# First layer of a hybrid decoder step: a third of the tokens runs ahead through the first feed-forward, and VectorE does the whole depthwise convolution

## The reference

```python
def swiglu(h, wg, wu, wd):
    return (jax.nn.silu(h @ wg) * (h @ wu)) @ wd

def conformer_conv(h, hist, w_pw1, b_pw1, w_dw, b_dw, ln_g, ln_b, w_pw2, b_pw2):
    u = h @ w_pw1 + b_pw1
    g = u[..., :D_CONV] * jax.nn.sigmoid(u[..., D_CONV:])
    gh = jnp.concatenate([hist.astype(g.dtype), g], axis=1)
    new_hist = gh[:, -CONV_HIST:]
    c = causal_dwconv(gh, w_dw, b_dw)          # 31 taps, each channel by itself
    c = jax.nn.silu(layernorm(c, ln_g, ln_b))
    return c @ w_pw2 + b_pw2, new_hist

# trunk, per layer i
    hn = rmsnorm(h, norm_mix[i])
    ... mix = conformer_conv(hn, ...) if i is even, ssd_mixer(hn, ...) if odd
    h = h + mix
    h = h + swiglu(rmsnorm(h, norm_ffn[i]), ffn_w_gate[i], ffn_w_up[i], ffn_w_down[i])
```

## Time and profile before

| what | value |
|---|---|
| median of 3 runs | 3497.72 us (3488.77 to 3501.15) |
| the profiled execution | 3490.01 us, its span 3488.1 us |
| PE busy | 3325.2 us, 95% of the span |
| DVE, ACT, POOL busy | 1591.4 (46%), 872.0 (25%), 934.1 us (27%) |
| granted TensorE clock, mean | 0.978 of full speed |
| read from memory | 131.39 MB |

### The profile page before, as it was taken

How to read it: one execution, slowest core, us unless ns; L and a number is a source line. 1 busy time by engine, 2 the same in 40 slices (tenths; PEclk the granted TensorE clock), 3 DMA queues, 4 the chain that set the end, 5 groups by cost and what they waited for, 6 DMA issues and landing times.

```text
span 3488.1 us, 52341 instructions
## 1 busy us (share of the span) xinstructions
PE 3325.2 (95%) x19646; PEld 3156.8 (91%) x19646; DVE 1591.4 (46%) x2619; ACT 872.0 (25%) x1570; POOL 934.1 (27%) x733
## 2 busy tenths in 40 slices
PE   4899969999999999998999999999979999999998
PEld 3888749999999999887999999999978999999998
DVE  3299962232222322646566575575654223222234
ACT  2111042211111111433333333333333111111113
POOL 2221122321111211413333334343333221112110
PEclk8999989999999999988999999999999999999999
DMA  3001001111111111110211211211111111111111
GB/s 99 25 25 30 18 5 41 43 42 46 44 42 42 42 48 42 43 46 11 59 45 36 63 50 37 63 32 49 48 35 31 42 42 48 42 42 42 44 46 58
DMA packets 226995, 147.24 MB, mean 42 GB/s; under 512 B 7796, under 2 KB 208852, under 8 KB 226866
## 3 DMA queue, kind: packets, MB, share of 16 engines
q1 hardware_dynamic: 226757, 145.96, 14.2%
q10 hardware_dynamic: 173, 0.39, 0.1%
HBM read 131.39 MB, written 15.65 MB: 42 GB/s over the span
## 4 chain that ended last, share of the span: by engine, by line
PE 83%; issue 6%; DVE 6%; ACT 2%; POOL 1%; DMA 1%; SPq 0%; DVEq 0%; POOLq 0%; ACTq 0%
PE bank L535 69%; PE bank L525 2%; PE bank L636 2%; PE bank L875 2%; PE bank L561 1%; PE bank L880 1%; PE bank L881 1%; PE bank L912 1%; PE bank L918 1%; DVE arena L1491 1%; DVE arena L1416 1%; DVE arena L1494 1%; DMA stage<-in_cf_w_pw 1%; PE bank L986 1%; DVE bank L1426 0%
## 5 line engine op out<-in xcount | busy, mean ns | idle before, releaser
L535 PE MATMUL bank<-xhi,whi 128*128 128x368 f32 x3840 | 1282.2, 334 | 33.5 <-POOL xlo L1875 25.3
L535 PE MATMUL bank<-xlo,whi 128*128 128x368 f32 x3840 | 1271.9, 331 | 0.0
L535 PE MATMUL bank<-xhi,wlo 128*128 128x368 f32 x3840 | 1269.0, 330 | 0.0
L1869 POOL TENSOR_TENSOR wlo<-stage,whi 128x1024 fp32r<-128x1024 f32 x220 | 544.5, 2475 | 1572.0 <-ACT whi L1028 1572.0
L535 PEld LDWEIGHTS bank<-xhi,whi 128*128 128x128 f32 x3840 | 724.8, 189 | 50.2 <-issue 31.8
L535 PEld LDWEIGHTS bank<-xlo,whi 128*128 128x128 f32 x3840 | 723.8, 188 | 3.5
L535 PEld LDWEIGHTS bank<-xhi,wlo 128*128 128x128 f32 x3840 | 724.2, 189 | 0.0
L1572 DVE TENSOR_TENSOR h<-h,bank 128x368 f32<-128x368 f32 x480 | 258.1, 538 | 684.0 <-PE bank L535 684.0
L535 PE MATMUL bank<-ahi,whi 128*128 128x368 f32 x1440 | 510.2, 354 | 0.0
L535 PE MATMUL bank<-ahi,wlo 128*128 128x368 f32 x1440 | 476.6, 331 | 0.0
L535 PE MATMUL bank<-alo,whi 128*128 128x368 f32 x1440 | 476.6, 331 | 0.0
(11 more groups left out here) (214 smaller groups left out, 2988.8 us busy)
## 6 DMA issues: line engine op xcount, KB each, us to landing
stage<-in_ssd_w_in SPq DMA_DIRECT2D x48, 512.0 KB, 3.9
stage<-in_ffn_w_gate SPq DMA_DIRECT2D x44, 512.0 KB, 3.7
stage<-in_ffn_w_up SPq DMA_DIRECT2D x44, 512.0 KB, 3.7
stage<-in_ffn_w_down SPq DMA_DIRECT2D x44, 512.0 KB, 3.5
stage<-in_cf_w_pw SPq DMA_DIRECT2D x24, 512.0 KB, 3.9
arena<-in_state_ssm SPq DMA_DIRECT2D x16, 512.0 KB, 4.5
out_ss_s<-arena SPq DMA_DIRECT2D x16, 512.0 KB, 3.5
stage<-in_ssd_w_out SPq DMA_DIRECT2D x16, 512.0 KB, 3.5
```

Of the source, the lines that this page charges most:

```text
L535: mm = pe.matmul(bank[b][:, 0:TC], w[:, slot, w0:w0 + P], x[:, k, cs], start=n == 0, stop=n == 3 * len(offs) - 1)
L1869: pool.tensor_tensor(wlo[:, slot, :], stage[:, slot, :], whi[:, slot, :].bitcast(F32), ALU.subtract)\
```

## The change

Chunk 0 goes ahead of the other two through the first layer. During pw1, VectorE does for each tile only the 304 prompt columns of chunk 0, all 31 taps (`conv_first`); two accumulators, for even and odd taps, lie in PSUM banks 6 and 7. The 64 sample columns are multiplied on POOL (`products`, 8 instructions of 8 x 31) and summed by one reduction on VectorE. Then LayerNorm, pw2 (8 products), RMSNorm and the whole FFN run for chunk 0 alone (66 products). In this time VectorE does the convolution of the other 736 tokens: 248 instructions (`taps`, 8 tiles by 31), whose accumulators lie in PSUM (banks 4 to 6, two tiles in turn by even and odd m) and whose last tap writes SBUF; they are dealt out by hand between the other work of VectorE. Then LayerNorm for chunks 1 and 2, pw2 (16 products), RMSNorm, and the FFN for these two chunks (132 products). The FFN's 66 units and the 8 of pw2 are so loaded and split twice; while chunk 0 is alone the units go around three slots. TensorE's taps, its diagonals and the tap sums on ACT are gone. The samples' history transposes of the SSD layer move into the second FFN pass.

```diff
+PW2B = [(0, 1)] + [x for m in range(KT - 1) for x in ((m + 1, 1), (m, 2))] + [(KT - 1, 2)]
+def front_products():
+    order = [(U_PW1 + 2 * m + v, ("pw1", m, v, c)) for m in range(KT) for v, c in pw1_order(m)]
+    order += [(U_PW2A + m, ("pw2", m, 0)) for m in range(KT)]
+    order += [(unit_first(x, 0, j), (x, 0, j)) for x in "gu" for j in range(2)]
+    for f in range(FP - 1):
+        order += [(unit_first("g", f + 1, j), ("g", f + 1, j)) for j in range(2)]
+        order += [(unit_first("d", f, k // 4), ("d", f, k)) for k in range(KT)]
+        order += [(unit_first("u", f + 1, j), ("u", f + 1, j)) for j in range(2)]
+    order += [(unit_first("d", FP - 1, k // 4), ("d", FP - 1, k)) for k in range(KT)]
+    order += [(U_PW2B + m, ("pw2", m, c)) for m, c in PW2B]
...
 # TensorE
+            first_gate(0)
+            first_up(0)
+            for f in range(FP - 1):
+                first_gate(f + 1)
+                first_down(f)
+                if f == FP - 3:
+                    for k in range(6):
+                        conv_mean(1, k, 7)
+                if f == FP - 2:
+                    for k in range(6, KT):
+                        conv_mean(1, k, 7)
+                    for k in range(KT):
+                        conv_mean(2, k, 4)
+                first_up(f + 1)
+            pe.wait_ge(cen_done, KT + 2)
+            add_squares(N_LN, 1, range(KT))
+            first_down(FP - 1)
+            add_squares(N_LN, 2, range(KT))
...
 # VectorE
-            def conv_tile(m, a, nt=CW - CT):
...
+            def conv_first(m):
+                glu_part(m, 0)
...
+                    else:
+                        dve.wait_ge(c_step, base + t - 1)
+                        out = conv_a[:, m, NS:TC] if t == CW - 1 else acc
+                        dve.scalar_tensor_tensor(out, src, w, acc, ALU.mult, ALU.add).then_inc(c_step, 1)
+                    if t == 14:
+                        glu_part(m, 1)
+                    elif t == 20:
+                        glu_part(m, 2)
+                    elif t == 27:
+                        dve.wait_ge(g_prod, m + 1)
+                        dve.tensor_reduce(conv_a[:, m, 0:NS].rearrange("p (b r) -> p b r", b=DB), prod,
+                                          mybir.AxisListType.X, ALU.add).then_inc(g_red, 1)
...
+            def taps(count):
...
+                    src, acc = glu[:, m, TC - NS + t:TC - NS + t + 2 * TC], conv_sum[:, m % 2 * 2 * TC:(m % 2 + 1) * 2 * TC]
...
+                        dve.wait_ge(d_step, q - 1)
+                        out = conv_bc[:, m, :] if t == CW - 1 else acc
+                        dve.scalar_tensor_tensor(out, src, w, acc, ALU.mult, ALU.add).then_inc(d_step, 1)
...
+            dve.wait_ge(tl_kept, 1)
+            taps(5)
+            invert(N_LN, 0)
+            ln_scale(0, 0)
+            ln_scale(0, 1)
+            taps(8)
+            for m in range(KT):
+                taps(2)
+                res(m, 0, N_FFN0)
+            taps(4)
+            invert(N_FFN0, 0)
+            scale(N_FFN0, 0, C_FFN, range(KT))
+            taps(10)
...
+            taps(4)
+            first_up(0)
+            for f in range(FP - 1):
+                taps(6 if f < FP - 2 else KT * CW)
+                if f == FP - 2:
+                    dve.wait_ge(d_step, KT * CW)
+                first_down(f)
+                if f == FP - 2:
+                    center(1)
+                    center(2)
+                else:
+                    taps(4)
+                first_up(f + 1)
+            invert(N_LN, 1)
+            ln_scale(1, 0)
+            ln_scale(1, 1)
+            first_down(FP - 1)
+            invert(N_LN, 2)
+            ln_scale(2, 0)
+            ln_scale(2, 1)
+            for m, c in PW2B:
+                res(m, c, N_FFN0)
...
 # GpSimd
-            def diagonals(m, a, t):
...
+                for t in range(DL):
+                    v = pool.tensor_tensor(prod[:, :, t, :], gsam[:, m, :, t:t + CW], wt.to_broadcast([P, DB, CW]), ALU.mult)
...
+            for m in range(KT):
+                products(m)
+                splits(U_PW1 + 2 * m)
+                if m == KT - 1:
+                    tails(m)
+                splits(U_PW1 + 2 * m + 1)
+                if m < KT - 1:
+                    tails(m)
```

More of the change, by code:

```diff
@@ L83, in hybrid_step, with down_bank, last_in @@
+def down_bank(cs, q):
+    return ([3 * j + c for j in range(2) for c in cs] + [b for b in range(6) if b % 3 not in cs])[q % 6]
+def last_in(cs, b):
+    return max(q for q in range(KT * len(cs)) if down_bank(cs, q) == b)
 def hybrid_step(nc, i, o):
@@ L394, in _ @@
[L394 to L402, removed]
+            for v in range(2):
+                cols(v, v, i["cf_w_pw1"][0], v * D)
@@ L645, in _ @@
             pe.wait_ge(x_kept[0], 9)
             pe.wait_ge(x_kept[1], 9)
[L647 to L656 removed]
+            for m in range(KT):
+                pw1(m)
+                if m == 0:
+                    history()
@@ L692, in _ @@
[L692 to L702 removed]
+            add_squares(N_LN, 0, range(KT))
@@ L1168, in _ @@
             for b in range(DB):
-                act.dma_start(o["cc_s"][0, b, HIST - DL:HIST, :], trow[32 + b * DL:32 + (b + 1) * DL, :]).then_inc(stored, 16)
-            norm(N_LN, conv, affine=True)
+                act.dma_start(o["cc_s"][0, b, HIST - DL:HIST, :].rearrange("r (j n) -> r j n", j=2),
+                              trow[32 + b * DL:32 + (b + 1) * DL, :, :]).then_inc(stored, 16)
+            for m in range(KT):
+                act.wait_ge(acc_done, DONE["pw2", m, 0])
+                splits(U_PW2A + m)
+                square_tile(N_FFN0, 0, m)
@@ L1451, in _ @@
+                invert(n, NC - 1)
+                scale(n, NC - 1, gain, range(KT))
             for q in range(1, 18, 2):
@@ new lines, in first_up, with first_down @@
+            def first_up(f):
+                first_act(f, 0)
+                taps(1)
+                first_lo(f, 0)
+                taps(2)
+                first_act(f, 1)
+                taps(2)
+                first_lo(f, 1)
+            def first_down(f):
+                for k in range(KT):
+                    dve.wait_ge(acc_done, DONE["d", f, k])
+                    hm = h[:, k, 0:TC]
+                    dve.tensor_tensor(hm, hm, bank[(2 + k) % 4][:, 0:TC], ALU.add).then_inc(f_down, 1)
+                    if k % 2:
+                        taps(1)
@@ new lines, in _ @@
+            lo_of(N_LN, 0, 0)
+            lo_of(N_LN, 0, 1)
+            for m in range(KT):
+                splits(U_PW2A + m)
+            lo_of(N_FFN0, 0, 0)
+            lo_of(N_FFN0, 0, 1)
+            for u in range(U_FIRST, U_PW2B - 2):
+                splits(u)
+            lo_of(N_LN, 1, 0)
+            lo_of(N_LN, 1, 1)
+            splits(U_PW2B - 2)
+            splits(U_PW2B - 1)
+            lo_of(N_LN, 2, 0)
+            lo_of(N_LN, 2, 1)
+            for m in range(KT - 1):
+                splits(U_PW2B + m)
```

948 lines of the change are left out of this document (545 added, 403 removed).

## The result

The changed kernel takes 3400.35 us (median of 4 runs, 3396.67 to 3401.14) against 3493.24 before (median of 4, 3488.0 to 3501.15; a fourth run, of 3488.0, moved the median of the three from 3497.72): ratio 0.973, 95% interval 0.9707 to 0.9754. The runs of the kernel before lie around 3488 and around 3500 us, so a few us against it mean little by themselves. The forecast was 3384 in 3340 to 3455: right in direction, mechanism and range, with the gain 20 us larger than measured. Profiled run against profiled run it is 3490.0 to 3396.7, 93.3 us, where 113.6 were forecast.

The account below looks back on a forecast made before the run. TensorE was taken as the bound: 239.3 us of non-product time less 125.7 us of added terms gave a gain of 113.6, so 3376 against the profiled 3490.0, or 3384 us on the median, range 3340 to 3455.

Parts of the forecast that it names:

- What bounds and what goes: Whole kernel: TensorE is the bound; from pw1's second tile to the FFN, 239.3 of 505.3 us aren't products and can be won.
- Price of a tap: VectorE's convolution: 0.90 us for 736 columns with a PSUM accumulator, bounds 0.75 and 1.67; 0.46 us for 304 columns.
- The prediction's 10 us for that rule: Chunk 0's FFN pass: would lose some 10 us if a PSUM source cost each tap an estimated 0.065 us more.
- VectorE under TensorE: Chunk 0's FFN pass: VectorE needs 23.1 us a pair beside TensorE's 24.2, 95%, so its work is hidden.
- rival (b)'s second mechanism: VectorE's taps stand still while POOL runs: nine pairs +120 us, pw1 +39, 46 slower; chance 0.09 for both (b) mechanisms.
- rival (c): Chunk 0's pass: weights streamed twice come every 5 us instead of 4.03, +72 us, 3448 (median 3456); chance 0.13.
- a turn of slots that TensorE waits on: Weight units going around the slots: TensorE waiting on them was named as making the prediction wrong; no size given.
- The piece of 25 taps: Last pair but one of chunk 0's FFN pass: taps take 22.5 us ahead of the additions; TensorE waits 14.5.
- square sums between products, 8 x 0.31: pw2 of chunk 0: eight square sums on TensorE at 0.31 us each add 2.5 us.
- LayerNorm of chunk 0: Between pw1 and pw2 of chunk 0: nothing covers this norm, which adds 36.3 us with hand-overs.
- End of the pass: After chunk 0's FFN: LayerNorm and pw2 square sums, reciprocal and scaling wait 6.5, xlo and two cold restarts add 25.7 us.
- The second FFN pass: FFN for chunks 1 and 2: the 16.9 us that the FFN had beyond its products stay unchanged.

## Why the prediction was right, and where its sum was off

- *What bounds and what goes*: right. TensorE now meets the 42 products of pw1 without waiting from the second tile on (121.09 to 294.5: 173.4 us for 169.3 of products).
- *Price of a tap*: 0.90 forecast, 0.89 measured, 0.44 for 304 columns (0.46). Neither bound was needed. By the Trainium skill's page "VectorE: DVE Perf Modes", section "The TRN2 errata", PSUM would be dearer by an estimated 0.065 us an instruction. Accumulators in SBUF gave 0.97 us for a tap alone and PSUM 0.98, start to start 0.89 in both, so this kernel shows no such difference. The prediction's 10 us for that rule don't come out of its own terms either: 19 taps make 1.2 us a pair, of which 1.1 was spare, so about 1 us in nine pairs.
- *VectorE under TensorE*: right, 92% busy where 95% was forecast; without its taps the pass lasts as long.
- *The lock, rival (b)'s second mechanism*: right to be set aside, and shown by moving the accumulators: 104.7 us in the pass, where the prediction had 120. The Trainium skill's page "SBUF — State Buffer", section "SBUF: two separate sides", names VectorE instructions in a 2-port mode beside those with two SBUF inputs. The addition of 64 columns, one input, SBUF to SBUF, agrees with that (2.40 us against 0.28), though no run shows which mode it ran in.
- *Weights, rival (c)*: no wait in the pass; the margin is one slot. But a turn of slots that TensorE waits on was one of the prediction's signs of being wrong, and there is one, in pw2's second pass.
- *The piece of 25 taps*: 13.7 against 14.5.
- *The sum*: 21.8 us short. The step that failed, by its size, is "square sums between products, 8 x 0.31". The row was ten matmuls of 0.31 us for five tiles: each sum, one call in the source on plain float32 tiles and not on the rounded ones of the products, is two matmuls. One tile's sum as the profile after shows it, between two products, and the next:

```profile
351.44 0.34 PE L665 MATMUL banks<-xhi,wlo 128*128 128x368 f32 x1
351.62 0.78 PE L691 MATMUL banks<-arena,mean_w 128*128 128x368 f32 x2
351.95 0.61 PE L665 MATMUL banks<-xhi,whi 128*128 128x368 f32 x1
...
356.26 0.78 PE L691 MATMUL banks<-arena,mean_w 128*128 128x368 f32 x2
```

From one such pair to the next, with 24 matmuls between, are 4.64 us (351.62 to 356.26), 0.61 more than a product. All terms with sums or means carried half the price, as leaving 18 sums out showed (11.6 us less): the means 2.0 + 3.1 became 3.4 + 5.9, the sixteen sums for LayerNorm of the others 5 became 9.3, those in pw2 5.0 became 7.4 for the twelve that stand between products. That is about half of the 21.8.
- *LayerNorm of chunk 0*: 4.3 too little with pw1's start; 2.1 of it is the addition of 64 columns that I had as a small one, the rest I put down to the means' price and a second matmul pair behind VectorE's last addition, which no run separates.
- *End of the pass*: besides the sums, one wait for wlo (4.0 us and 2.4 for the cold clock) that the forecast didn't have, since it took the slots' turn as even where the last two units break it (exchanging them, with the splits moved, took 6.6 us off); the wait behind reciprocal and scaling came out at 3.85 instead of 6.5.
- *The second FFN pass*: taken as unchanged ("the 16.9 us that the FFN had beyond its products"), and 5 us too cheap. At its last products the two profiles are 91.5 us apart, at the first product of the second layer 86.2. In the norm there TensorE waits 2.6 us for a down addition and 1.9 us for nothing that the profile shows, where before it waited 0.8 us in all.

So the table's sum agrees with the 93.3 us between the profiled runs in part by luck: these 5 us are lost behind its last row, and some 7 come back in the second layer, which wasn't touched. What stays open is where these 7 come from: there the two profiles are between 82 and 94 us apart, and their ends 93.2.

## What to carry to other kernels

Where one engine is the bound by its busy share, split that share into the work that must be done and the rest, stage by stage, and look for a part of the work that can run ahead as cover for the engine that is late; loading weights a second time cost TensorE one wait of 4.0 us here and none in the pass itself. Place the accumulators of a long VectorE chain in PSUM, so that each instruction has one SBUF input, if POOL is busy beside it. And count the instructions in a row before taking its mean as the price of an operation: one call in the source may be two on the engine.

## What the runs showed of the hardware that was not expected

- Beside a POOL instruction that reads SBUF, a VectorE instruction of one SBUF input and SBUF output can stand still as well: an addition of 64 columns took 2.40 us, and 0.28 from PSUM. The first tap of a tile, a TENSOR_SCALAR of 736 columns, took 0.66 us from SBUF to SBUF with POOL idle and 2.6 in four of the five cases that met a POOL instruction; into PSUM it took 1.05 with POOL idle or busy. The last tap, with one input in SBUF and one in PSUM, took 0.97 us on average although it writes SBUF.
- The standing still goes both ways: beside taps with two SBUF inputs POOL's split took 2.884 us on average instead of 2.393.
- With POOL idle the accumulator's place made no difference: taps of 736 columns started 0.89 us apart in PSUM and in SBUF.
- A square sum on plain float32 tiles was two matmuls, 0.61 us between products, where a matmul on the rounded tiles took 0.17 us start to start at full clock.
